# Each expert slab loaded as two transfers of half its columns, both counted on the slab's semaphore

## What is computed

```python
def _swiglu(h, wg, wu, wd):
    return (jax.nn.silu(h @ wg) * (h @ wu)) @ wd

def _moe(h, router, wg, wu, wd):
    ...
    top_v, top_i = lax.top_k(logits, TOP_K)          # 2 of 8 experts for each token
    ...
    for e in range(N_EXPERTS):
        y = y + combine[..., e:e + 1].astype(h.dtype) * _swiglu(h, wg[e], wu[e], wd[e])
    return y
```

## Time and profile before

| | us |
|---|---|
| median of three runs | 1537.03 (1533.57 to 1537.9) |
| the profiled execution | 1543.62 |
| its span, first to last instruction | 1541.8 |
| PE busy | 1504.5 (98% of the span) |
| the expert passes, PE's first gather product to its last down product | 1130.87 to 1527.72 |
| DMA queue q1 (SP's): 268.10 MB | 47.2% of 16 engines' span |
| DMA queue q8 (instructions): 143 packets, 2.34 MB | 0.6% |

### The profile page before, as it was taken

One profiled execution on the slowest core, in us unless ns is written; L12 is line 12 of the kernel. 1 busy time (PEld: TensorE's weight loads), 2 busy tenths in 40 slices (PEclk: granted clock), 3 DMA queues, 4 the chain that ended last, 5 costly groups with the idle time before them and its releaser, 6 DMA issues.

```text
span 1541.8 us, 41139 instructions
## 1 busy us (share of the span) xinstructions
PE 1504.5 (98%) x18219; PEld 1289.5 (84%) x18219; DVE 711.0 (46%) x1568; ACT 337.0 (22%) x841; POOL 56.3 (4%) x68
## 2 busy tenths in 40 slices
PE   9999999999999999999999999999989999999887
PEld 6899976887779999998899867877778897888665
DVE  6446666634245656565467467542241221222213
ACT  2314224122112222133233232230120000000001
POOL 1000010100000000000000010200010000000000
PEclk9999999999999999999999999999999999999999
DMA  8324344212634444347326352116788899999991
GB/s 328 126 88 169 143 146 119 84 43 73 245 131 143 149 155 163 111 153 305 120 91 232 114 133 92 54 46 242 301 298 328 327 337 349 337 340 331 349 418 69
DMA packets 64332, 299.82 MB, mean 194 GB/s; under 512 B 21839, under 2 KB 23567, under 8 KB 37663
## 3 DMA queue, kind: packets, MB, share of 16 engines
q1 hardware_dynamic: 50392, 268.10, 47.2%
q0 software_dynamic: 2944, 18.09, 3.1%
q10 hardware_dynamic: 10823, 11.05, 2.7%
HBM read 277.93 MB, written 19.28 MB: 193 GB/s over the span
## 4 chain that ended last, share of the span: by engine, by line
PE 93%; DVE 3%; issue 2%; DMA 1%; ACT 1%; SPq 0%; DVEq 0%; ACTq 0%
PE ps L1721 15%; PE ps L1871 15%; PE ps L1132 12%; PE ps L1595 11%; PE ps L1803 7%; PE ps L1602 6%; PE ps L1659 4%; PE ps L1081 4%; PE ps L1094 2%; PE ps L1451 2%; PE ps L1754 2%; DMA ring<-in_mix 1%; PE ps L1147 1%; PE ps L1427 1%; PE ps L1185 1%
## 5 line engine op out<-in xcount | busy, mean ns | idle before, releaser
L1595 PE MATMUL ps<-xn,ring 128*128 128x288 f32 x768 | 203.0, 412 | 0.8 <-DMA ring<-in_mix 0.4
L1595 PEld LDWEIGHTS ps<-xn,ring 128*128 128x128 f32 x768 | 142.0, 190 | 48.6 <-issue 11.7
L1721 PE MATMUL ps<-y_ml,arena 128*64 128x96 f32 (+5 forms) x3584 | 143.8, 243 | 15.5 <-issue 15.5
L1721 PEld LDWEIGHTS ps<-y_ml,arena 128*64 128x64 f32 x3584 | 140.6, 141 | 20.4 <-issue 20.1
L1871 PE MATMUL ps<-arena 128*128 128x144 f32 x1028 | 133.4, 285 | 0.9 <-DVE arena L3189 0.9
L1871 PEld LDWEIGHTS ps<-arena 128*128 128x128 f32 x1028 | 129.3, 189 | 1.0 <-issue 1.0
L1803 PE MATMUL ps<-arena,mixed 128*32 128x256 f32 x2024 | 113.0, 383 | 0.6 <-issue 0.6
L3137 DVE TENSOR_TENSOR mixed<-ps,mixed 128x96 f32<-128x96 f32 (+5 forms) x88 | 21.7, 247 | 187.5 <-PE ps L1721 187.3
L1803 PEld LDWEIGHTS ps<-arena,mixed 128*32 128x32 f32 x2024 | 75.5, 111 | 35.1 <-issue 3.1
L1721 PEld LDWEIGHTS ps<-y_ml,ring 128*64 128x64 f32 x2048 | 80.9, 140 | 12.3 <-issue 12.2
L1721 PE MATMUL ps<-y_ml,ring 128*64 128x64 f32 (+5 forms) x2048 | 84.6, 243 | 5.6 <-issue 5.6
(11 more groups left out here) (531 smaller groups left out, 2217.3 us busy)
## 6 DMA issues: line engine op xcount, KB each, us to landing
arena<-in_egu SPq DMA_DIRECT2D x56, 1024.0 KB, 6.1
ring<-in_mix SPq DMA_DIRECT2D x46, 1024.0 KB, 5.3
arena<-in_edown SPq DMA_DIRECT2D x40, 1024.0 KB, 6.1
ring<-in_mix SPq DMA_DIRECT2D x48, 768.0 KB, 4.2
ring<-in_egu SPq DMA_DIRECT2D x32, 1024.0 KB, 6.9
ring<-in_gu SPq DMA_DIRECT2D x14, 1024.0 KB, 4.8
arena<-in_gu SPq DMA_DIRECT2D x8, 1024.0 KB, 5.0
arena<-in_C POOLq DMA_DIRECT2D x2, 2048.0 KB, 7.9
```

The lines of the kernel that those rows point to most:

```text
L1595: last = mm(ps[:, bank, 0:T], ring[:, s, P * k:P * k + P], xn[:, k, :], start=(k == 0), stop=(k == KT - 1))
L1721: last = mm(out(r), stationary(r), moving, start=start, stop=stop, skip_group_check=True)
```

## The change

SP issues two transfers for each expert slab in place of one: columns 0 to 1023 of all 128 partitions, then columns 1024 to 2047 (512 and 512 for the last slab of an expert). In each partition a transfer now moves 4 KB instead of 8 KB (2 KB instead of 4 KB for the last slab). Both add 16 to the slab's semaphore, and the three places that count them, PE's wait and SP's wait for the slab two before, count 32 where they counted 16. The dense layer's loads, which share six of the semaphores, and the mixer's loads are as they were. No wait is added or taken away, and the order of the slabs is the same. A slab is used when both of its halves have landed.

```diff
@@ block.sync
+                def in_halves(k, width, src):
+                    for c in (slice(0, width // 2), slice(width // 2, width)):
+                        sp.dma_start(eslab(k)[:, c], src[:, c]).then_inc(e_ld[k].sem, 16)
+
                 def first_expert(slabs):
                     for k in slabs:
-                        src = a["egu"][k] if k < FT else a["edown"][k - FT, :, 0:D * len(DOWN[k - FT])]
-                        sp.dma_start(eslab(k), src).then_inc(e_ld[k].sem, 16)
+                        width = SLOT if k < FT else D * len(DOWN[k - FT])
+                        in_halves(k, width, a["egu"][k] if k < FT else a["edown"][k - FT, :, 0:width])
...
-                            sp.wait_ge(e_ld[j].sem, p * 16 + (16 if k >= IN_FLIGHT else 0) + expert_loads(j))
+                            sp.wait_ge(e_ld[j].sem, p * 32 + (32 if k >= IN_FLIGHT else 0) + expert_loads(j))
...
-                        sp.dma_start(eslab(k)[:, 0:width], src.rearrange("a p n -> p (a n)")).then_inc(e_ld[k].sem, 16)
+                        in_halves(k, width, src.rearrange("a p n -> p (a n)"))
@@ block.tensor
-                pe.wait_ge(e_ld[k].sem, p * 16 + 16 + expert_loads(k))
+                pe.wait_ge(e_ld[k].sem, p * 32 + 32 + expert_loads(k))
```

## The result

The changed kernel takes 1558.97 us (median of 4 runs, 1554.85 to 1562.66) against 1535.30 us for the kernel before (4 runs, 1531.58 to 1537.9). The ratio is 1.0151, with a 95% interval of 1.0124 to 1.0177: 1.5% slower, some 23 us. The forecast was 1528.6 us, with a range of 1520 to 1540. The time is near that of the rival called the stream becomes the bound, 1557.5 us.

A forecast was written before the change was run, and what follows sets the result against it. PE was taken to be bound by waits for instruction fetches, not weights. Shorter gaps without and under the limit, clock and mixer's slab: -4.1 - 2.9 - 1.5 + 0.1 = -8.4 us, from 1537.03 to 1528.6 us; range 1520 to 1540.

The forecast's parts named there:

- the stream becomes the bound: Passes 1 to 6, SP's issue chain: over 0.16 us more a slab makes the last slab late; 1557.5 us, chance 0.13.
- What bounds the kernel, and the slack: Expert passes: PE waits for instruction fetches, not weights; the stream of slabs has 18.8 us of slack.
- Packets of 4 KB: Expert slabs' stream: smaller packets add 0.03 us a slab (at most 0.34), 3.6 us over 119 slabs, hidden by slack.
- Twice the issues on SP: SP's queue: a second issue of 0.33 us a slab, made while the first half moves, costs the stream nothing.
- What a fetch meets on its engine: PE's instruction fetches: 8.4 packets pass ahead, now in 1.5 us, each fetch up to 1.1 us sooner; -4.1 and -2.9 us.
- the rival of bytes: Instruction fetches: engines let through a number of bytes, so fetches wait as before; 1537.1 us, chance 0.35 (or nothing changes).
- The mixer's slab: PE's 12.04 us wait for the last mixer slab: three expert slabs ahead add 0.1 us, at most 1.0.
- The lower clock: PE's clock falls after the longest gaps; with shorter gaps one of three slow stretches goes, -1.5 us.

The follow-up runs named there:

- the second profile: The changed kernel, unaltered, measured and profiled again beside later runs: 1562.92 us, 1.0134 times the kernel before, 3.47 us a slab.
- the halves outside the limit: Changed kernel with halves only in the first expert and the last pass, whole slabs in passes 1 to 6: 0.9994 times the kernel before.
- quarters: Changed kernel with each slab as four transfers of a quarter of its columns, on one semaphore: 1594.43 us.
- large part first: Changed kernel with unequal parts, seven eighths of a slab's columns first, then the last eighth: 1542.90 us, 1.0009 times the kernel before.

## Why the prediction was wrong

**What bounds the kernel, and the slack: right.** PE didn't wait for slabs, and a third slab under way without halves changes nothing. The gaps come after 126 or 127 matmuls or after three times as many (the one of 1495.72), not always after 127 or 128, which changes nothing. The slack of 18.8 us held, but not the 0.16 us a slab: that divides by 119 slabs, of which the 17 of the last pass aren't under the limit. By 102 it is 0.18 us, and PE's waits for slabs begin between 3.27 and 3.29 us a slab, 0.17 to 0.19 over before.

**Packets of 4 KB: right.** Forecast +0.03 us a slab, hidden; the single transfer with such packets has +0.03, as near as two profiles can tell, and no loss of time. The upper bound, +0.34, was too high: where no limit holds, two transfers and smaller packets together are +0.10.

**Twice the issues on SP: wrong, and this is the step that decided.** It said "the second half is issued while the first (1.3 us of data) moves. Behind it on SP are only the next slab's waits", and costed the stream at nothing. That SP has the time is true, and beside the point. The limit of two under way makes a loop: issue, landing of the whole slab, next issue. The semaphore counts both halves, so the later one's landing closes the loop, 0.52 us (not the 0.33 of the earlier trace rows, since the registers are set again in between) after the first is issued. The sum should have asked what a later last issue does to the landing; I asked only whether the engines have data. By the loop it is 0.52 / 2 = 0.26 us a slab if the latency of the last part stays what it was, and it did (5.95 us against 6.01): 102 x 0.26 - 18.8 = +7.7 us. The measured 0.28 gives +9.8 and the 0.37 of the second profile +18.9, against spans that are 11.2 and 23.6 us longer than that of before. In place of a gain of 8.4 us the medians show a loss of 23.7.

The rival had the place right, and got a chance of 0.13. That its time came so near, 1557.5 us, is in part luck: its price was an issue of 0.33 us in series for each slab, over 119 slabs. Over the 102 that the limit holds back it gives 33.7 - 18.8 = +14.9 us, 1551.9.

The Trainium skill (DMA: Bandwidth & Descriptors, section Rules for kernel authors) asks for 128 partitions and 1 MiB or more in a DMA for maximum bandwidth. The rows agree, with a small size: where no limit holds, a slab takes 2.60 us in halves of 512 KB and 2.50 whole. That isn't the 1.5%, as the halves outside the limit cost no time. The same section says not to bother with two transfers to disjoint partition halves, since both use the same 16 engines. That row is on halves by partitions, which lost 13.6% here, and not on halves by columns.

**What a fetch meets on its engine: wrong, and this was the forecast's gain.** It went by a count of 8.4 packets that pass ahead of a fetch. In the last pass of after PE resumes at 1514.36 and the next fetch starts between 1518.0 and 1518.2 us, in this view of the queues:

```profile
q1 hardware_dynamic: 18, 0.07, 86.8%
q8 instruction: 1, 0.02, 34.7%
```

That is 3.7 us, as before with packets of 8 KB, and not 2.6. The four such waits in the pass are 3.68 to 3.79 us. With quarters, packets of 2 KB, PE resumes at 1551.34 and the fetch starts between 1555.1 and 1555.2; the waits are 3.81 to 3.89. So no count of 8.4 packets sets the wait, and the rival of bytes (or of a time) fits on this term. Bytes and a fixed time can't be told apart here. The expected cut of 1.1 us in each gap didn't come: the gaps of 1512.08 and 1518.30 are 2.28 us, the longest before in the unlimited part 2.05.

The Trainium skill's rule of turns at packet granularity (the same page, section Queues, rings and completion order), which I took to speak for a count, has packets that are groups of descriptors. The records show pieces of 8, 4 or 2 KB, the fetch waits as long behind each, and how they are grouped no row shows. So these rows go against a count of such pieces, and they don't test the rule.

**The mixer's slab: the size was off.** Forecast 0.1 us, bound 1.0. The wait is

```profile
1063.73 12.78 DMA ring<-in_mix
```

against 12.04, 0.7 us more. It cost nothing, as PE reaches its first expert product at 1130.93 us, before at 1130.87, and the kernel with halves outside the limit, which has it too, is as fast as before.

**The lower clock: no gain.** It hung on shorter gaps. In the last stretch it is 0.96 against 0.95, with waits for slabs in the place of others, and 0.91 in the second profile of after; no more can be said from these.

**The chances.** What failed was the weighing too: the whole of the forecast rested on a mechanism of which the text says "no row of before shows it directly", while the loop of issue and landing stood in the earlier trace rows, 90.1 us of waits of SP for slabs in one row alone and 0.4 for PE.

## What to carry to other kernels

Where a limit on transfers under way makes the issuing queue wait for landings, cost an added transfer by the loop (separation of its issues, latency of the last one, time to the next issue, divided by the number under way), and not by whether engine or queue have room. A separate semaphore and limit for each part, or one more under way, took PE's waits for slabs away here, but left 0.8% and 0.4% of the time; a small last part (one eighth) lost nothing that could be measured. And ask of a stream that isn't the bound by how much: 0.18 us a slab was all that stood between no wait for slabs and a loss of 1.5%.

## What the runs showed of the hardware

- With one slab of 1 MB under way, a last part of 128 KB behind the other 896 KB of its slab lands 5.76 us after its issue, and a whole slab of 1 MB 6.01 us after its own (large part first, and before).
- Transfers of 64 partitions by 8 KB move 219 GB/s over 1200 to 1460 us against 339 of whole ones (second stretch of before, above), and their packets take 0.57 us, those of 128 partitions 0.31:

```profile
DMA packets 9081, 56.91 MB, mean 219 GB/s; under 512 B 1778, under 2 KB 1778, under 8 KB 2554
...
q1 hardware_dynamic: 8594, 54.75, 95.0%
```

- An instruction fetch of 16 KB starts 3.7 to 3.9 us after PE resumes when the queue of slabs is full, whether the packets ahead of it have 8, 4 or 2 KB (last pass of before, after and the quarters), and 1.1 us after it when the last slab has landed.
- The first packet of a transfer on an engine is longer than those behind it. With the packets strung on the 16 engines by their ends and starts (1220 to 1450 us), the first of a slab takes some 510 to 550 ns in the mean, by how closely ends and starts have to meet, and the fourth to eighth 315 to 320, in the kernel before. With packets of 4 KB in one transfer it is 260 to 310 against about 165.
